# A layer's recurrence in 32x32 blocks: the doubling levels of a two-layer kernel on compact blocks in four row groups

## What is computed

```python
def step(state, inp):
    r_t, d_t, k_t, v_t, kk_t, a_t = inp
    sa = jnp.einsum('bhvk,bhk->bhv', state, kk_t)
    state = (state * d_t[:, :, None, :] - sa[..., None] * (kk_t * a_t)[:, :, None, :]
             + v_t[..., None] * k_t[:, :, None, :])
    return state, jnp.einsum('bhvk,bhk->bhv', state, r_t)

seq_major = lambda t: jnp.swapaxes(t, 0, 1)
inputs = (seq_major(rh), seq_major(decay), seq_major(kh), seq_major(vh), seq_major(kk), seq_major(ah))
_, y = lax.scan(step, jnp.zeros((b, hh, n, n), jnp.float32), inputs)
```

## Time and profile before

| what | value |
|---|---|
| median of 3 runs | 1392.91 us (1391.98 to 1393.37) |
| the profiled execution, its time | 1387.37 us |
| its span, first to last instruction | 1385.6 us |
| mean granted TensorE clock | 0.992 of full speed |
| TensorE busy | 1344.1 us, 97% of the span |
| recurrence, first `grams` to the output projection | 745.5 us to 845.2 us |

### The profile page before, as it was taken

One profiled execution on the slowest core, in us unless ns is written; L12 is line 12 of the kernel. 1 busy time (PEld: TensorE's weight loads), 2 busy tenths in 40 slices (PEclk: granted clock), 3 DMA queues, 4 the chain that ended last, 5 costly groups with the idle time before them and its releaser, 6 DMA issues.

```text
span 1385.6 us, 24728 instructions
## 1 busy us (share of the span) xinstructions
PE 1344.1 (97%) x10364; PEld 779.2 (56%) x10364; DVE 436.5 (32%) x982; ACT 271.4 (20%) x533; POOL 93.9 (7%) x124
## 2 busy tenths in 40 slices
PE   7999999999999999979999998999999999999997
PEld 6889443444434444339688998944444443434433
DVE  2245122222222222146652337622222222222213
ACT  1231211111111111112421331121111111111111
POOL 7202000000000000012003100300000000000001
PEclk9999999999999999999999999999999999999999
DMA  4697799999999999975323006679999999999993
GB/s 152 178 358 310 305 364 408 422 422 422 421 422 422 422 422 422 421 251 171 115 101 124 4 4 245 258 292 374 398 422 422 422 422 422 422 422 421 422 420 156
DMA packets 98666, 450.45 MB, mean 325 GB/s; under 512 B 16032, under 2 KB 45344, under 8 KB 48928
## 3 DMA queue, kind: packets, MB, share of 16 engines
q1 hardware_dynamic: 98592, 449.34, 80.9%
HBM read 448.26 MB, written 1.05 MB: 324 GB/s over the span
## 4 chain that ended last, share of the span: by engine, by line
PE 93%; DVE 5%; issue 1%; DMA 1%; ACT 1%; POOL 0%; SPq 0%; DVEq 0%; PEldq 0%; ACTq 0%
PE PS L1882 31%; PE PS L1921 17%; PE PS L1929 10%; PE PS L1853 7%; PE PS L549 4%; PE PS L512 3%; PE PS L1396 2%; PE PS L1373 2%; PE PS L1358 2%; PE PS L1901 1%; PE PS L1521 1%; PE PS L2002 1%; PE PS L1536 1%; PE PS L1545 1%; PE PS L1893 1%; PE PS L534 1%
## 5 line engine op out<-in xcount | busy, mean ns | idle before, releaser
L2234 DVE TENSOR_TENSOR y_parts<-PS,y_parts 128x512 fp32r<-128x512 f32 x128 | 88.5, 691 | 216.7 <-ACT y_parts L2136 216.7
L2208 DVE SCALAR_TENSOR_TENSOR AR<-AR,PS 128x256 f32<-128x256 f32 x64 | 30.8, 481 | 386.5 <-ACT AR L2114 386.5
L1929 PE MATMUL PS<-y_parts,token_map 128*128 128x512 f32 x496 | 146.6, 417 | 0.0
L1882 PE MATMUL PS<-AR,xT 128*64 128x512 f32 x512 | 115.7, 593 | 5.6 <-issue 5.5
L1929 PEld LDWEIGHTS PS<-y_parts,token_map 128*128 128x128 f32 x496 | 83.5, 188 | 60.9 <-issue 50.3
L1921 PE MATMUL PS<-AR 128*64 128x512 f32 x512 | 116.9, 598 | 0.0
L1921 PE MATMUL PS<-RING,AR 128*64 128x512 f32 x496 | 116.9, 598 | 0.0
L1882 PE MATMUL PS<-AR 128*64 128x512 f32 x512 | 115.5, 592 | 0.0
L2136 ACT CAST y_parts<-PS 128x512 fp32r<-128x512 f32 x128 | 75.0, 586 | 172.0 <-PE PS L1921 172.0
L1882 PE MATMUL PS<-RING,xT 128*64 128x512 f32 x480 | 108.1, 592 | 0.0
L1882 PE MATMUL PS<-RING,AR 128*64 128x512 f32 x480 | 108.1, 592 | 0.0
(11 more groups left out here) (315 smaller groups left out, 1575.7 us busy)
## 6 DMA issues: line engine op xcount, KB each, us to landing
RING<-in_moe_w_gate SPq DMA_DIRECT2D x64, 1024.0 KB, 11.8
RING<-in_moe_w_up SPq DMA_DIRECT2D x64, 1024.0 KB, 13.9
AR<-in_moe_w_gate SPq DMA_DIRECT2D x64, 1024.0 KB, 13.2
AR<-in_moe_w_up SPq DMA_DIRECT2D x64, 1024.0 KB, 15.2
AR<-in_moe_w_down SPq DMA_DIRECT2D x64, 1024.0 KB, 14.0
RING<-in_moe_w_down SPq DMA_DIRECT2D x62, 1024.0 KB, 15.1
AR<-in_ab_w_in SPq DMA_DIRECT2D x8, 1024.0 KB, 5.6
AR<-in_rw_w_o SPq DMA_DIRECT2D x4, 1024.0 KB, 5.3
```

The source lines that it names most:

```text
L1882: ins = nc.tensor.matmul(PS[s * B:(s + 1) * B, 4, :], gathered(k)[:, c:c + B], gate_and_up(slots[s])[:, k, :, :], start=(k == 0), stop=(k ...
L1929: ins = nc.tensor.matmul(PS[:, 2 * t + h, :], OHT[:, half, t, :], YS[:, n, h * 512:(h + 1) * 512], start=False, stop=True, skip_group_chec ...
L2208: nc.vector.scalar_tensor_tensor(out=HH[0:2 * B, :].rearrange("p (k j) -> p k j", k=FT), in0=by_row(SIL[0:2 * B, :]), scalar=GC[:, buf:buf ...
L2234: nc.vector.tensor_tensor(YS[:, 1, h * 512:(h + 1) * 512], PS[:, 5 + h, :], YS[:, 0, h * 512:(h + 1) * 512], ALU.subtract).then_inc(q["low ...
```

## The change

All levels work on two 32x32 blocks on the diagonal of each 64x64 system, as level 5 already worked on one block. The middle factor, the inverse and its transpose are stored compactly, 32 columns for each pair of heads in place of 64 (`HB`), in PSUM as in SBUF. A matmul of 64x64 becomes two of 32x32 in different row groups of the array, so that the four groups are used in turn. Level 5 uses the same matmuls as before. The old `DT` is only written at the end of level 4 (its lower block under a mask `islow`, one more ACT operation for each chunk) and at level 5; between levels the transposed inverse stands in a new tile `DC`.

```diff
-                cols = slice(0, 32 if lv == LEVELS else CH)
-                V.tensor_tensor(dst[:, :, cols], bank(4 * w)[:, :, cols],
-                                SM[:, lv:lv + 1, cols].to_broadcast([P, KT, cols.stop]),
-                                ALU.mult).then_inc(r[f"factor_ready{w}"], 1)
+                V.tensor_tensor(dst, PS[:, 4 * w, 0:KT * HB].rearrange("p (k t) -> p k t", k=KT),
+                                SM[:, lv:lv + 1, :].to_broadcast([P, KT, HB]), ALU.mult).then_inc(r[f"factor_ready{w}"], 1)
...
-                    A.copy(DG[w], bank(4 * w)).then_inc(r[f"inverse_ready{w}"], 1)
+                    A.copy(DG[w], blocks(4 * w)).then_inc(r[f"inverse_ready{w}"], 1)
                 s.wait_ge(r[f"turned_inverse_done{w}"], LEVELS * wave + lv)
-                cols = slice(32 if lv == LEVELS else 0, CH)
-                A.copy(DT[c][:, :, cols], bank(4 * w + 1)[:, :, cols]).then_inc(r[f"turned_inverse_ready{w}"], 1)
+                if lv == LEVELS - 1:
+                    A.activation(DT[c][:, :, own[0]], blocks(4 * w + 1), ACT.Copy, scale=islow[:, 0:1])
+                dst = DT[c][:, :, own[1]] if lv == LEVELS else DC[w]
+                A.copy(dst, blocks(4 * w + 1)).then_inc(r[f"turned_inverse_ready{w}"], 1)
...
                     else:
-                        ins = mm(PS[rows, 4 * w, col(k)], GMB[c][rows, k, 0, :],
-                                 DG[w][rows, k, :] if lv else ident[rows, rows], start=True, stop=True)
+                        for rows, cols in zip((lo, hi), own):
+                            ins = mm(PS[rows, 4 * w, blk(k)], GMB[c][rows, k, 0, cols],
+                                     DG[w][rows, k, :] if lv else ident[rows, rows], start=True, stop=True)
...
                 if lv < LEVELS:
                     for k, h in core:
-                        rows = token_rows(h, c)
-                        ins = mm(PS[rows, 4 * w, col(k)], DT[c][rows, k, :], XI[w][rows, k, :], start=True, stop=True)
+                        for rows, cols in zip((lower[(c % 2) ^ h], upper[(c % 2) ^ h]), own):
+                            ins = mm(PS[rows, 4 * w, blk(k)], known(rows, k, cols), XI[w][rows, k, :], start=True, stop=True)
                     ins.then_inc(r[f"inverse_done{w}"], 1)
...
-                        ins = mm(PS[rows, 4 * w + 1, col(k)], XI[w][rows, k, :], DT[c][rows, k, :], start=True, stop=True)
+                        for rows, cols in zip((lo, hi), own):
+                            ins = mm(PS[rows, 4 * w + 1, blk(k)], XI[w][rows, k, :], known(rows, k, cols),
+                                     start=True, stop=True)
...
-            for pair in range(2):
-                for n in range(2):
-                    grams(pair, n)
+            grams(0, 0)
+            grams(0, 1)
+            for n in range(4):
+                turn(n)
             product(0, 0)
+            grams(1, 0)
             product(1, 0)
```

More of the change, by code:

```diff
@@ L39 @@
 CH = 64
+HB = CH // 2
 NCH = T // CH
@@ L105, in program @@
         MKC = sb("MKC", [P, 2, CH])
-        SM = sb("SM", [P, LEVELS + 1, CH])
+        SM = sb("SM", [P, LEVELS + 1, HB])
         SMT = sb("SMT", [P, CH])
         E64 = sb("E64", [P, CH])
+        islow = sb("islow", [P, 1])
         m01 = sb("m01", [P, T])
@@ L286, in program @@
         LG = take(D)
-        DG = [take(KT, CH) for _ in range(2)]
-        XI = [take(KT, CH) for _ in range(2)]
+        DG = [take(KT, HB) for _ in range(2)]
+        XI = [take(KT, HB) for _ in range(2)]
+        DC = [take(KT, HB) for _ in range(2)]
         KTK = [take(KT, P) for _ in range(TT)]
@@ L625, in constants @@
             link(nc.gpsimd.tensor_copy(identb, ident[:, :]))
+            link(nc.gpsimd.memset(islow[:, :], 1.0))
+            link.sync()
+            for n in (1, 3):
+                link(nc.gpsimd.memset(islow[HB * n:HB * n + HB, :], 0.0))
+            link.sync()
             link(nc.gpsimd.memset(iotab[:, CAP:B], 4.0 * T))
@@ L847, in program @@
         core = [(k, h) for k in range(KT) for h in range(2)]
-        lower = [slice(0, 32), slice(CH, CH + 32)]
-        upper = [slice(32, CH), slice(CH + 32, P)]
+        blk = lambda k: slice(k * HB, (k + 1) * HB)
+        lower = [slice(0, HB), slice(CH, CH + HB)]
+        upper = [slice(HB, CH), slice(CH + HB, P)]
+        own = [slice(0, HB), slice(HB, CH)]
         first_part = [(0, 0), (0, 1), (1, 0), (1, 1)]
@@ L1097, in dve_core @@
                 masked(*g)
[L1098 to L1118, removed]
+            for lv in range(LEVELS + 1):
                 factor(0, lv)
                 factor(1, lv)
+                masked(*masked_order[4 + 2 * lv])
+                masked(*masked_order[5 + 2 * lv])
             factor(2, 0)
@@ L1221, in act_core @@
             bank = lambda b: PS[:, b, :].rearrange("p (k t) -> p k t", k=KT)
+            blocks = lambda b: PS[:, b, 0:KT * HB].rearrange("p (k t) -> p k t", k=KT)
             def turned(n):
@@ L1252, in deviation @@
                 A.activation(RS[:, t, :], RS[:, t, :], ACT.Sqrt).then_inc(r["deviation_ready"], 1)
-            for lv in range(1, LEVELS):
+            for n in range(4):
+                turned(n)
+            for lv in range(1, LEVELS + 1):
                 inverse(0, lv)
                 inverse(1, lv)
[L1257 to L1260, removed]
             for n in range(4, 8):
@@ L1310, in gp_mix1 @@
                 r["gate_weights_copied"], 1)
-            for c in range(2):
+            for c in range(0, NCH, 2):
                 unit(g, c)
-            for c in range(2):
+                unit(g, c + 1)
                 seed(g, c)
+                seed(g, c + 1)
             g.wait_ge(r["bonus_ready"], 1)
@@ L1324, in gp_mix1 @@
                 G.tensor_tensor(RES[:, t, :], RES[:, t, :], LB, ALU.add).then_inc(r["residual_ready"], 1)
[L1325 to L1328, removed]
         def unit(g, c):
@@ L1495, in grams @@
                 m, part = n // 2, n % 2
+                if pair == 1 and n < 2:
+                    pe.wait_ge(r["turned_copied"], 3 + n)
                 for k in range(4 * part, 4 * part + 4):
@@ L1514, in product @@
                 for k, h in core:
-                    rows = token_rows(h, c)
+                    lo, hi = lower[(c % 2) ^ h], upper[(c % 2) ^ h]
                     if lv == LEVELS:
-                        lo, hi = lower[(c % 2) ^ h], upper[(c % 2) ^ h]
-                        ins = mm(PS[hi, 4 * w, k * CH:k * CH + 32], GMB[c][lo, k, 0, 32:CH], DG[w][lo, k, 0:32],
-                                 start=True, stop=True)
-                    else:
-                        ins = mm(PS[rows, 4 * w, col(k)], GMB[c][rows, k, 0, :],
-                                 DG[w][rows, k, :] if lv else ident[rows, rows], start=True, stop=True)
+                        ins = mm(PS[hi, 4 * w, blk(k)], GMB[c][lo, k, 0, own[1]], DG[w][lo, k, :], start=True, stop=True)
+                    else:
+                        for rows, cols in zip((lo, hi), own):
+                            ins = mm(PS[rows, 4 * w, blk(k)], GMB[c][rows, k, 0, cols],
+                                     DG[w][rows, k, :] if lv else ident[rows, rows], start=True, stop=True)
                 ins.then_inc(r[f"product_done{w}"], 1)
@@ L1549, in turn @@
                 t, m, part, b = n // 4, n % 4 // 2, n % 2, (2, 3, 6, 7)[n % 4]
[L1550 to L1553, removed]
+                if n >= 4:
+                    pe.wait_ge(r["gram_masked"], masked_by((n // 2, 2 + n % 2)))
                 for k in range(4):
@@ L1643, in loaded @@
                 pe.wait_ge(s_rw[(2, 3, 0, 1)[c]], RW0[(2, 3, 0, 1)[c]] + 16 * 4)
-            for pair in range(2):
-                for n in range(2):
-                    grams(pair, n)
+            grams(0, 0)
+            grams(0, 1)
+            for n in range(4):
+                turn(n)
             product(0, 0)
+            grams(1, 0)
             product(1, 0)
-            grams(0, 2)
+            grams(1, 1)
             product(0, 1)
@@ L1653, in pe_core @@
             inverse(0, 1)
+            inverse(1, 1)
+            grams(0, 2)
+            product(0, 2)
+            product(1, 2)
             grams(0, 3)
[L1655 to L1658, removed]
             inverse(0, 2)
-            grams(1, 3)
             inverse(1, 2)
@@ L1663, in pe_core @@
             product(1, 3)
+            grams(1, 2)
             inverse(0, 3)
@@ L1667, in pe_core @@
             product(1, 4)
-            turn(0)
-            turn(1)
+            grams(1, 3)
             inverse(0, 4)
             inverse(1, 4)
-            turn(2)
-            turn(3)
             product(0, 5)
             product(1, 5)
-            turn(4)
-            turn(5)
             inverse(0, 5)
             inverse(1, 5)
-            turn(6)
-            turn(7)
+            for n in range(4, 8):
+                turn(n)
             product(2, 0)
```

16 lines of the change are left out of this document (8 added, 8 removed).

## The result

The changed kernel takes 1438.91 us (median of 4 runs, 1434.99 to 1442.16) against 1392.45 us of the kernel before (4 runs, 1388.90 to 1393.37): 1.0337 times as long, 95% interval 1.0305 to 1.0370. The forecast was 1439.

What follows compares the result with a forecast made beforehand. Bound taken: instruction fetch, one piece of 127.4 pairs per 3.75 us, with the array at its limit too. +47.0 us for the pieces less 0.5 for the start is +46.5; 1392.9 + 46.5 = 1439 us, range 1425 to 1454.

Steps and rivals of the forecast that it cites:

- The pieces: TensorE's program in the recurrence: 1664 more pairs at 127.4 per fetched piece make 13.06 more pieces.
- the sum: Recurrence from 755.10 to 832.05: 33.06 pieces x 3.75 us = 124.0, less 76.95, gives +47.0 us.
- the stated range: Recurrence stretch: +42.1 us with a 3.6 us cycle to +52.0 with 3.9; whole kernel 1425 to 1454 us.
- The cycle: A starved TensorE in the recurrence gets one piece of program every 3.75 us, the mean over 16 packets.
- the signs that were named: Profile after: 74 packets 3.6 to 3.9 us apart, issue stops of 1 to 2.5 us, output projection near 891 us.
- The array at 0: Recurrence blocks: array time, at most 2.3 us for two blocks, lies inside the 3.75 us cycle; counted 0.
- DVE and ACT at 0: Recurrence factors and copies on half the columns run while PE waits for program; counted 0.
- The start, -0.5 us: Recurrence start: the 1.53 us mask wait goes, first piece ends earlier; -0.5 us, between -1.3 and 0.
- The clock rival: Recurrence: TensorE's clock falls to 1.2 GHz, adding 13 to 26 us, around 1458 us; chance 0.06.
- half of it or less inside the fetch's cycle: Clock rival's step: of 26 us for 885 unchanged pairs, half or less is hidden, leaving 13 to 26 us.
- The rule of the Trainium skill: Instruction fetch: crossing 16 KiB blocks is mostly hidden; by it the change would be worth the first rival's -19 us.

Runs made afterwards that it cites:

- The loop: Kernel before with 832 unused 32x32x32 matmuls ahead of the first grams, as a loop of 13 rounds of 64: 1405.0 us, ratio 1.0122.
- the straight line: Kernel before with 832 unused 32x32x32 matmuls ahead of the first grams, written as straight code: 1438.33 us, ratio 1.0339.
- e8_changed: The changed kernel itself, measured and profiled a second time: 1441.6 us (1436.33 to 1445.34).
- the two row groups: Changed kernel with each block's matmuls ordered lower halves first, then upper, so two row groups alternate, not four: 1443.39 us.
- The kernel with the order alone: Kernel before, keeping its 64x64 blocks, in the changed kernel's order on every engine: 1389.0 us, ratio 0.9982.
- The loop of levels: Changed kernel with levels 2 to 4 of the first pair of chunks as a loop of three rounds, four small matmuls added per round: 1426.55 us.
- the fillers: Changed kernel with two unused 128x128x256 matmuls ahead of each of the 52 blocks: 1443.41 us, ratio 1.0386 to the kernel before.

## Why the prediction was right

*The pieces.* 13.06 more were forecast and 13 more packets came. The loop against the straight line shows the cause. The stretch of 33.06 pieces was to take 124.0 us and took 123.6 in the first profile, 128.7 in the second (e8_changed): +46.7 and +51.8 against the +47.0 of the sum, and +46.5 and +50.4 for the medians of the whole kernel. The two sets are 4 us apart, so that the first came within 0.3 us of the sum is luck; that both lie in the stated range is not.

*The cycle.* 3.75 us was right as a mean, 123.6/33.06 = 3.74 and 128.7/33.06 = 3.89, but single pieces vary. Those that have a stop at both ends, 21 of them, took 3.28 to 4.11 us, 3.6 on average, most of them 3.45 to 3.6:

```profile
775.78:779.89 4.11, 1.34 (x127) 1.23 (x128) 0.00 (x0) 0.75 (x2) 1.28 (x1) 0.89 0.01 4
817.71:820.99 3.28, 2.45 (x129) 2.27 (x128) 1.24 (x3) 0.00 (x0) 0.00 (x0) 1.00 0.02 5
```

In the straight line, where nothing else happens, they took 3.45 to 4.00 us. So 3.38, the shortest distance of before, does occur, but not as a mean. The other 12 pieces come in six stretches of two without a stop between; they took 48.0 us, 4.0 each. Among them are 808.93 to 817.71, 8.78 us with TensorE busy 7.35 (transposes and 64-wide blocks at a clock of 0.76), and the last two of the stretch, where the array and not the fetch is the limit:

```profile
872.29:881.68 9.39, 9.39 (x253) 9.14 (x254) 4.43 (x34) 4.51 (x8) 0.00 (x0) 0.51 0.03 6
```

Of the signs that were named, the 74 packets and the stops are there. The stops take 0.3 to 2.9 us, not 1 to 2.5, and the projection starts at 894.9 us, not 891, 3.0 us of it because this execution's recurrence starts later.

*The array at 0.* Right, and tested by the two row groups. Four groups are faster than two, as the grams had made likely: in the changed kernel 62 loads of a block take 0.67 us at the full clock (776.01) and 64 take 1.00 at the lower one (765.67). The 0.6 us that was foretold for a block holds.

*DVE and ACT at 0.* Right: between 758.1 and 881 us no wait of TensorE is ended by DVE or ACT in the view of waits; every one ends with "issue", here the largest group (us in total, times, longest):

```profile
PEld PS L1536 <- issue: 16.3, 10, 2.1
```

*The start, -0.5 us.* From the first `grams` to the first stop's end it is 9.57 us before and 9.50 after: -0.1. The wait for the masks is gone, but the piece after it comes no sooner: 2.74 us of "issue" until 758.04 stand in its place. Data movement from 752 to 760 us in slices of 0.2 us:

```profile
GB/s 400 358 328 338 348 225 328 246 143 287 389 430 389 389 430 369 205 82 20 82 0 0 0 0 0 0 0 0 0 0 0 0 0 0 0 82 0 0 0 0
```

The piece's packet starts between 755.8 and 756.0 us, when the weights' transfers have ended. The prediction had named this ("its packet must have come, and DMA is busy there") and counted too little for it; that the transfers hold the packet back is not tested. The kernel with the order alone has no such stop there, and keeps 2 us of gain.

*The clock rival.* It happened, and its price was too high. The prediction gave it 0.06, since the clock was full in all of the recurrence before; it is 0.67 in the stretch after. Blocks of 64 columns do take nearly twice as long (1.58 us for 32 loads at 769.43 against 0.86 at 772.97), but most of that lies inside the wait for the next piece, and the low clock does not lengthen a starved cycle: 3.45 to 4.00 us in the straight line at 0.50, 3.76 to 3.99 in the kernel before at 1.00. The low clock costs where TensorE has no stop, as in the last two pieces above. As an estimate, the 12 pieces without a stop between them took 48.0 us, 5 more than at the others' 3.6 us, so the clock's price is some 5 us at the most, not 13 to 26. The failed step of this rival is "half of it or less inside the fetch's cycle": of its 26 us some 21 or more were. Those 5 us are in the 3.74 us of the mean, so part of the agreement of 3.75 with 3.74 is chance.

*What the skill says.* The rule of the Trainium skill that was weighed ("Runtime: NRT & Kernel Launch", section Instruction fetch mechanics: crossing a block is mostly hidden) does not hold for TensorE here: 3.73 us for new program against 1.41 us for repeated. The same section says that a taken branch out of the current window of two pages forces a fetch. The loop of levels does not agree: it jumps back over 392 pairs, 3.1 pieces, and no packet starts in rounds two and three.

## What to carry to other kernels

A matmul has a price in instructions beside the one in columns: in this kernel 28 to 31 ns for each pair of weight load and matmul that is new program, however small the tile. Where the profile shows PEld stopping at "issue" every 127 or 128 loads, as here, cutting tiles smaller makes TensorE slower even if the array is faster on them. Count pairs first, and look at whether the stretch can be a loop: repeated code had no such limit (11 ns a pair in the loop of small matmuls).

## What was unexpected of the hardware

- The clock falls where TensorE is starved. In the changed kernel it first fell in the recurrence just behind the stop that ends at 758.04, and over the 123.6 us, with TensorE busy 88.4, it was 0.67, which is a change between 2.4 and 1.2 GHz. It was 0.50 in the straight line of small matmuls from 750 to 792 us (busy 21.8 of 42 us), and 1.00 with the fillers (busy 50.7 of 54 us). The busy time alone does not tell: with two row groups in turn the clock was 0.50 although TensorE was busy 41.7 of 45 us.

```profile
755.00:800.00 45.00, 41.69 (x1558) 39.00 (x1554) 8.12 (x16) 5.94 (x16) 13.36 (x8) 0.50 0.02 5
```

- TensorE keeps at least three pieces of its program for repetition, though it brings only one ahead: rounds two and three of the loop of levels, 3.1 pieces long, ran without a packet.
- The jump of a loop is cheap: weight loads pause 0.23 us between two rounds (1.18 + 0.23 = 1.41 us).
